# An encoder layer on one Trainium2 core: in the attention, ScalarE's side work is issued behind the copy of the transposed weights

## The reference, cut to what matters

```python
s = jnp.einsum('bhcqd,bhckd->bhcqk', qblk, k) * scale      # two score matrices, c = 0, 1
p = jax.nn.softmax(s, axis=-1)
a = p[:, :, 0] - lam * p[:, :, 1]
o = jnp.einsum('bhqk,bhkv->bhqv', a, v)                     # attention output, then rmsnorm per head
s = jnp.einsum('bhncd,bhnmd->bhncm', qc, kc) * mask         # retention, computed here without chunks
y = jnp.einsum('bhncm,bhnmv->bhncv', s, vc)                 # then rmsnorm per head, times silu(gr)
```

## Time and profile before

| | us |
|---|---|
| median of 3 runs | 1220.36 (1219.81 to 1221.09) |
| profiled execution, its own time | 1215.92 |
| span of the profile, first to last instruction | 1214.1 |
| TensorE busy in it | 1098.5 (90%) |
| VectorE busy | 521.2 (43%) |
| ScalarE busy | 402.1 (33%) |
| attention stage, 357.0 to 469.3 of the span | 112.3 |

### The profile page before, as it was taken

One profiled execution on the slowest core, in us unless ns is written; L12 is line 12 of the kernel. 1 busy time (PEld: TensorE's weight loads), 2 busy tenths in 40 slices (PEclk: granted clock), 3 DMA queues, 4 the chain that ended last, 5 costly groups with the idle time before them and its releaser, 6 DMA issues.

```text
span 1214.1 us, 15517 instructions
## 1 busy us (share of the span) xinstructions
PE 1098.5 (90%) x5148; PEld 664.9 (55%) x5148; DVE 521.2 (43%) x893; ACT 402.1 (33%) x629; POOL 189.5 (16%) x236
## 2 busy tenths in 40 slices
PE   5899999999989889999987999999998798998960
PEld 4688888888876657778874333333333232333320
DVE  5651522111037887554344444443353334242418
ACT  5322233222135556212214143333244323333232
POOL 0110010101100000000000223223233323222220
PEclk9999999999999999999996999999999999999995
DMA  8633331621350004549349799999999999999546
GB/s 312 250 125 118 114 121 51 257 80 52 130 205 21 2 1 142 170 127 366 138 179 420 314 375 419 420 420 420 419 415 419 421 421 419 420 421 419 231 159 263
DMA packets 69248, 308.89 MB, mean 254 GB/s; under 512 B 9024, under 2 KB 9152, under 8 KB 43872
## 3 DMA queue, kind: packets, MB, share of 16 engines
q1 hardware_dynamic: 56144, 273.86, 56.7%
q0 software_dynamic: 13072, 34.63, 7.3%
HBM read 278.57 MB, written 39.06 MB: 262 GB/s over the span
## 4 chain that ended last, share of the span: by engine, by line
PE 73%; DMA 11%; DVE 8%; ACT 4%; issue 3%; SPq 0%; DVEq 0%; ACTq 0%; POOLq 0%; POOL 0%
PE ps L865 19%; PE ps L580 12%; PE ps L582 12%; PE ps L581 12%; PE ps L892 9%; DMA rawe<-in_w 7%; PE ps L855 2%; PE ps L874 1%; DMA xg<-xn_scratch,idxt 1%; PE ps L672 1%; DMA xrow<-in_x_sample 1%; ACT cur L1188 1%; PE ps L653 1%; PE ps L785 1%; DMA ya<-y_scratch 1%
## 5 line engine op out<-in xcount | busy, mean ns | idle before, releaser
L580 PE MATMUL ps<-whi,xTh 128*128 128x512 f32 x480 | 188.6, 393 | 18.1 <-DVE wlo L1219 13.7
L581 PE MATMUL ps<-wlo,xTh 128*128 128x512 f32 x480 | 188.0, 392 | 0.0
L582 PE MATMUL ps<-whi,xTl 128*128 128x512 f32 x480 | 187.9, 392 | 0.0
L865 PE MATMUL ps<-cur13a,xT 128*64 128x512 f32 x656 | 155.3, 617 | 1.0 <-DVE xT L1633 0.8
L1656 DVE COPY cur13a<-rawe 128x4096 f32 x31 | 71.2, 2297 | 190.0 <-DMA rawe<-in_w 106.8
L865 PE MATMUL ps<-cur13b,xT 128*64 128x512 f32 x656 | 147.8, 592 | 0.0
L892 PE MATMUL ps<-cur,hT 128*64 128x512 f32 x640 | 146.2, 598 | 0.0
L1188 ACT ACTIVATE cur<-rawe 128x4096 f32 x31 | 112.2, 3619 | 3.6 <-issue 1.4
L580 PEld LDWEIGHTS ps<-whi,xTh 128*128 128x128 f32 x480 | 91.0, 190 | 37.6 <-issue 18.5
L959 ACT ACTIVATE zst<-ps,rstd 128x512 f32<-128x512 f32 x60 | 41.4, 693 | 207.8 <-PE ps L582 205.7
L581 PEld LDWEIGHTS ps<-wlo,xTh 128*128 128x128 f32 x480 | 91.1, 190 | 18.9
(11 more groups left out here) (212 smaller groups left out, 1396.2 us busy)
## 6 DMA issues: line engine op xcount, KB each, us to landing
rawe<-in_w SPq DMA_DIRECT2D x96, 2048.0 KB, 26.7
raw<-in_w_in SPq DMA_DIRECT2D x20, 1024.0 KB, 6.6
z_scratch<-zst POOLq DMA_DIRECT2D x60, 256.0 KB, 2.3
gat<-z_scratch SPq DMA_DIRECT2D x12, 512.0 KB, 3.9
xn_scratch<-rrow POOLq DMA_DIRECT2D x6, 1024.0 KB, 5.3
ya<-y_scratch SPq DMA_DIRECT2D x6, 1024.0 KB, 10.7
raw<-in_w_out SPq DMA_DIRECT2D x4, 1024.0 KB, 6.7
xcol<-in_x_cols SPq DMA_DIRECT2D x6, 512.0 KB, 9.9
```

Of the source, the lines that this page charges most:

```text
L580: pe.matmul(out, ah, bh, start=first, stop=False)
L581: pe.matmul(out, ah, bl, start=False, stop=False)
L582: return pe.matmul(out, al, bh, start=False, stop=last)
L865: mm = pe.matmul(ps[0][u * CAP:(u + 1) * CAP, :], xT[:, c, h * CAP:(h + 1) * CAP], cur13[h][:, :, c * 512 + u * 256:c * 512 + u * 256 + 25 ...
```

## The change: what it does

On ScalarE, attT(n) now stands directly behind `exps(n+1)` at every step where a head's squares, a high part or scalings are due; these come behind it. The lone square of a step within a head stays ahead of attT(n). `merge_hi(1)` moves from step 17 to step 18. On VectorE, `merge_lo(0)` moves from step 10 to 11 and `merge_lo(1)` from step 18 to 22. No instruction is added or removed on any engine, and TensorE, SyncE and GpSimd keep their order.

```diff
@@ ScalarE @@
             for n in range(NIT):
                 if n + 1 < NIT:
                     exps(n + 1)
-                if n == 9:
-                    merge_hi(0)
-                elif n == SAMPLE_END + 1:
-                    merge_hi(1)
-                elif n in (20, 21):
-                    normalise(1, 2 * (n - 20))
-                    normalise(1, 2 * (n - 20) + 1)
-                if 2 <= n < NIT - 1:
+                if 2 <= n < NIT - 1 and not last_of_head(n - 2):
                     squares(n - 2)
                 act.wait_ge(s_aT, n + 1)
                 if n >= 2:
                     act.wait_ge(s_o, n - 1)
                 w = SEQ_NT[ITS[n][0]] * P
                 act.activation(attT[n % 2][:, 0:w], ps[4][:, 0:w], ACT.Copy).then_inc(s_aTc, 1)
+                if 2 <= n < NIT - 1 and last_of_head(n - 2):
+                    squares(n - 2)
+                if n == 9:
+                    merge_hi(0)
+                elif n == SAMPLE_END + 2:
+                    merge_hi(1)
+                elif n in (20, 21):
+                    normalise(1, 2 * (n - 20))
+                    normalise(1, 2 * (n - 20) + 1)
@@ VectorE @@
-                if n == 10:
+                if n == 11:
                     merge_lo(0)
-                elif n == SAMPLE_END + 2:
-                    merge_lo(1)
                 elif n == SAMPLE_END + 3:
                     norms(1)
                 elif n in (20, 21):
                     normalise(1, 2 * (n - 20))
                     normalise(1, 2 * (n - 20) + 1)
+                if n == 22:
+                    merge_lo(1)
```

## The result

| | before | after |
|---|---|---|
| median of the runs, us | 1220.09 (1218.46 to 1221.09, 4 runs) | 1208.58 (1207.38 to 1209.09, 4 runs) |
| ratio, with its 95% interval | | 0.9898 [0.9885, 0.9912] |
| profiled execution, its own time | 1215.92 | 1208.70 |
| span of the profile | 1214.1 | 1206.9 |
| first scores to the value products of step 23 | 110.00 | 100.87 |

The kernel is faster by 1.0%, 11.5 us between the medians. Compared twice more, the same changed kernel came out at 0.9927 [0.9907, 0.9947] (1210.96, 4 runs) and 0.9924 [0.9905, 0.9943] (1209.93, 6 runs), so the gain is about 10 us. Both of these times lie inside the forecast's range. What is to be explained is one to two and a half us over the forecast.

What follows compares the result with a forecast made beforehand. The prediction took two nearly equal loops to bound the attention stage, TensorE's (4.33 us per 512-wide step) and VectorE with ScalarE's (4.12); gains summed place by place to 8.9, so 1220.36 - 8.9 = 1211.5 us, range 1209 to 1216.

Steps and rivals of the forecast that it cites:

- check from the other side: Attention stage: 11.8 us of waiting plus 5.8 of slow products, less 8 to 9 of remaining waits, is about 9.
- The sum place by place: Attention stage replayed on the trace's time axis, step by step, to a gain of 8.9 us at its end.
- Steps 5 and 13: Head ends: squares hidden, scores(8) and (16) at full clock; gain so far 2.0 us after step 5, 4.3 by step 16.
- Steps 9 to 12: exponentials(11) 0.4 us late behind the high part, merge_lo(0) costs 1.9 in step 11; gain so far 3.0.
- Steps 17 to 19, 21 and 22: merge_lo(1) leaves step 18: gain so far 7.3 us, 7.5 by step 21, 8.9 at the end with 0.9 cover.
- Rival 3: Step 22: late merge_lo(1) holds att(23) past the transposes by 2 us; gain 7; chance 0.22 together with rival 1.
- Rival 1: Attention stage keeps as many slow clock stretches; gain 5.5 to 7.5 us, time about 1214; chance 0.22 together with rival 3.
- rival 4: Slower: short waits swing the clock all through the stage; at mean clock 0.80, time 1232 us; chance of slower 0.02.
- a larger gain: Whole kernel: a gain above the forecast's 7.5 to 10.5 us, up to 12; chance 0.04.

Runs made afterwards that it cites:

- the rest alone: Against the kernel before: high parts, scalings and both low parts placed as in the change, head-end squares left ahead of the copy attT; 0.9939 (1214.57 us).

## Why the prediction was right, and where it was wrong

**The waits.** Right. The prediction asked for no wait for attT over 1.5 us; the longest is 0.6. How many short waits stay was wrong, and with it the "check from the other side". It put the waits for attT that stay at "8 to 9 in all" and took all 5.8 us of slow products as gone: 11.8 + 5.8 less 8 to 9 is about 9. Measured: 4.8 stay for attT and 1.2 come up for smk, so the waits give back 5.8 and not 3; the slow products give back 3.3 of TensorE's busy time and not 5.8, since those behind the wait of 2.8 us at step 0 stay ("in my sum all these slow products are gone" holds for the later ones only). The two errors cancel, and that this check came to 9 was luck. The sum place by place doesn't rest on it.

**Steps 5 and 13.** Right. Squares hidden, scores(8) at full clock, maxima(8) and (16) without a wait: 0.09 and 0.01 us from the forecast.

**Steps 9 to 12.** Right, with the cost too: exponentials held up behind the high part, reciprocal(12) held up by the low part.

**Steps 17 to 19, 21 and 22.** Right. The end of the stage is on TensorE, with the weights of step 23 ready at 456.4 and their transposes at 457.30: 0.9 us of cover, as forecast. Rival 3 did not occur.

**The rivals on the clock.** Rival 1 (the clock falls somewhere else) and rival 4 (short waits make it swing) did not occur: thirteen waits of up to 0.6 us for attT, and in the six later profiles of the changed order (three as it is, three with the first gap filled), as in the first, no group at half clock behind the first steps. The Trainium skill ("TensorE: Matmul & The Clock Gate", "A second HAM failure mode: psum-queue depth-cycling") would have many short idles make the clock swing. This case's trace doesn't show that at waits of 0.2 to 0.6 us: the granted clock of the stage is 0.97 to 0.98, and 1.00 with the first gap filled.

**The step that failed** is the last one of the sum: "The median of the runs is 4.4 above the profiled one, so the same gain gives 1220.36 - 8.9". The gain isn't the same in both. The slow products that the sum takes away came from one execution, in which the clock had fallen less than it mostly does: 0.94 over the stage, and 0.91 in three of the five profiles. In that profile the stage was 110.00, in the mean of five profiles 111.59; of the 4.4 us between the profiled run and the median, about 1.6 were more slow products in the very stage that the change repairs, and of these the change takes away the part that stands behind the later gaps. Another 1.1 is in the experts' part (509.64, and 510.7 in the mean of the five), which it leaves alone. The rest, 1.7, isn't found in one stretch: the five profiles' own times have a mean of 1219.09, 1.3 under the median of the forecast. With the gain of a usual execution the forecast would have been about 10 us and 1210.4, beside 1208.58, 1210.96 and 1209.93. The range leaned the wrong way by the same step: its lower end allowed a gain of 11.4, and "a larger gain" got 0.04, though the profile lay 4.4 us under the median and part of that could be in the stage.

This step explains one us of the 2.6 by which the first comparison missed the forecast. The gain of 11.5 there is more than the traces explain: 9.95 is the difference of the mean stages, 9.8 and 10.1 are the later differences of medians. What is left over, 1.5 us, I take for the spread of four runs; no run shows that. So the forecast's range was missed by 0.4 us in the first comparison in part by bad luck, and held in the two later ones.

Open is why the kernel before falls into one or the other pattern of slow groups. That it does is shown by five profiles; what decides it is not.

## What to carry to other kernels

Replay the places of a change on the trace's own axis, with starts and not durations: a sum made so held to 0.32 us over ten places. But look first whether the profiled execution is a usual one: where its time and clock differ from the median's, find out which stretch the difference is in, and if it is the one that you change, it belongs to the gain. Work that nobody waits for goes behind the copy that the bound engine waits for, and its price is then only what it has over the engine's next idle stretch.

## What the runs showed of the hardware

- After a gap of 1.3 to 2.1 us of TensorE the next groups run at 1.2 GHz (scores 2.08 instead of 1.13) in some executions and at 2.4 GHz in others, at the same place of the same kernel: behind the 1.62 at step 5 in four of five profiles, behind the 2.1 at step 9 in one, behind the 1.33 at step 20 in three. Behind the gap of 2.8 at step 0 groups are slow in all five, in a stretch of some 4 us or of some 7. The Trainium skill ("TensorE: Matmul & The Clock Gate", "What's actually happening") says of cold starts that the number of slow products varies from run to run; here the number varies for gaps in the middle of a kernel too, and between the profiles with a short and with a long slow stretch at the start the stage differs by 2.9 us of 110.
- Idle products in the gaps hold the clock at 1.00 over the whole stage, and the time of the kernel before falls by 0.34% and 0.43% in two comparisons, though TensorE does more.
- A 128x128 product call in fp32 costs 0.24 us of TensorE at 2.4 GHz (4.29 for 18), and one call is two products in the trace.
- Side work moved off the path in two halves was worth 0.62% and 0.61% alone and 1.0%, 0.7% and 0.8% together: at steps 9 and 17 the second half finds part of its gap already used, and some of the rest alone is the draw of the clock.
